# Low parts of the weights made earlier in DVE's order around three seams of a hybrid decoder layer

## The chip, the cores and the metric

The kernel runs on one core of one Trainium2 chip. The metric is device time in microseconds (us) of one execution; the figure of record before the change is 2464.99 us, the median of 3 runs (2464.16 to 2465.22).

## The reference

One inference step of one decoder layer with two branches, on 512 prompt tokens and 64 sample tokens (576 columns), width 2048, all in float32:

```python
h = rmsnorm(x, norm_g)
proj = einsum('bld,dp->blp', h, w_in)          # gates, conv inputs, q, k, v, forget code
za = cB * conv3(cC * cx) * silu(cg)            # branch A: short gated conv
branch_a = einsum('blc,cd->bld', za, w_branch_a)
o, S_new = gla_chunked(q, k, v, log_a, state)  # branch B: gated linear attention
zb = rmsnorm(o, gla_norm_g) * silu(gg)
branch_b = einsum('blv,vd->bld', zb, w_branch_b)
merged = sigmoid(ga) * branch_a + sigmoid(gb) * branch_b
x = x + einsum('bld,de->ble', merged, w_out)
y = rmsnorm(x, final_norm_g)
```

## The kernel before

TensorE computes everything in float32 by splitting each operand in a rounded high part and the remaining low part, and by taking three passes: high x high, high x low, low x high.

The first 715 us or so hold the attention work. What follows is the **pair stage**: 76 pairs of output tiles. Each pair is computed with a seven-product scheme of the Strassen kind (`NPROD = 7`), so there are 532 products, numbered `g = 7 * u + p` (u is the pair, p the product in it). Each product is 8 k-tiles times 3 passes, 24 matmuls of 128x128 by 288 columns. The pairs come in four phases:

- pairs 0 to 51: the projection, whose operand is h;
- pairs 52 to 59 (from `PAIR_A` = 52): branch A, `w_branch_a`;
- pairs 60 to 67 (from `PAIR_B` = 60): branch B, `w_branch_b`, with the merge;
- pairs 68 to 75 (from `PAIR_C` = 68): the output product, `w_out`.

At each of the three **seams** (52, 60, 68) the operand on the token side changes: seven new operand blocks are loaded or made, and ACT and DVE split them while the products run. In the first pair of a phase TensorE waits later than elsewhere (`late`): it starts a product with the high parts alone, and needs the weights' low part after 8 matmuls and a new operand's low part after 16. In all other pairs a product needs the weights' low part at its start.

The weights of product g go this way. SP loads four pieces of a pair (a11, a21, a12, a22). For p = 1, 2, 4, 5 DVE adds or subtracts two pieces first (`add_pieces`, L1973, L1978, L1980, L1982). ACT rounds the piece to its high part (`split_hi`, L1087) into a ring of three buffers; a buffer comes free when product g - 3 is done. DVE subtracts to get the low part (`split_lo`, L1963). Piece buffers come free when the low part is made, and SP waits for that count (`part_lo`) before it loads the next pair's pieces.

All engines run their orders as written. ACT's order for iteration g: save a product of the pair from PSUM (`save`, L1289), then `split_hi(g + 2)`, then splits of operands (L1417, L1345) and, around branch B, `slice_hi` (L1327), which waits for what DVE's stage made (`c_made`). Products 2, 4, 5 and 6 of a pair wait until an earlier product of it is saved (`part_saved`).

DVE's order for iteration g, while TensorE runs product g:

1. the stage's arithmetic on product g - 1, for p - 1 from 3 to 6 (`branch_a` L2470 to L2487, `branch_b` L2508 to L2546, `out_pair` L2588, L2591);
2. `add_pieces(g + 3)`, where that product needs a sum;
3. `split_lo(g + 2)`;
4. low parts of new operands (L2652; at seam C `rest_lo`, L2572), slices of branch B (L2553, L2560), the output rows (L2600).

In the output phase `turn_out` puts five transposes on TensorE in front of product 1 of each pair from 69 on; they wait for the stage's arithmetic on product 5 of the pair before (`c12_read`).

Of the kernel before, what the change touches and what calls it, by code (L numbers as in the profile page):

```python
# [46 lines left out]
NPROD = len(PRODUCTS)  # L47
# [22 lines left out]
PAIR_A, PAIR_B, PAIR_C = PAIRS_G, PAIRS_G + PAIRS_B, PAIRS_G + 2 * PAIRS_B  # L70
# [13 lines left out]
C_LO = ((2, 0, 3, 7), (4, 1, 0, 7), (5, 0, 7, 8), (6, 1, 7, 8), (7, 2, 7, 8), (8, 3, 0, 8), (9, 4, 7, 8), (10, 5, 0, 8),  # L84
        (11, 6, 0, 8))
# [4 lines left out]
NG = NPAIR * NPROD  # L90

def hybrid_kernel(nc, x_prompt, x_sample, state_conv, state_gla, norm_g, w_in, conv_w, w_alpha2,
# [51 lines left out]
    with ctx:  # L144
# [305 lines left out]
        def slot_of(slot, b, f32=False):  # L450

            if isinstance(slot, int):
                return (x_f32 if f32 else act_x)[:, slot, 1 - b, :, :]
            kh, j = int(slot[1]) - 1, int(slot[2]) - 1
            return (y_f32 if f32 else act_y)[:, kh * KH:(kh + 1) * KH, b, j * HALF:(j + 1) * HALF]
# [6 lines left out]
        def split_count(f, p):  # L462


            return 4 + NPROD * f + list(SPLITS[f].values()).index(p) + 1

        def phase_of(u):

            return (u >= PAIR_A) + (u >= PAIR_B) + (u >= PAIR_C)
# [22 lines left out]
        def kind_of(u):  # L492

            return FIRST[u][0] if u < PAIR_A else "branch" if u < PAIR_C else "out"
# [12 lines left out]
        def closed_before(u):  # L507

            return sum(closing[:u])
# [1343 lines left out]
        def _(dve):  # L1853
# [57 lines left out]
            for t in range(NT + 1):  # L1911
# [9 lines left out]
                n = P if t < NT else TS  # L1921
# [37 lines left out]
            def split_lo(g):  # L1959

                u, p = g // NPROD, g % NPROD
                dve.wait_ge(part_hi, g + 1)
                V.tensor_tensor(ring_lo[g % RING][:, :], piece_of[SOURCE[p]][u % 2][:, :],  # L1963
                                ring_hi[g % RING][:, :].bitcast(F32), ALU.subtract).then_inc(part_lo, 1)

            def add_pieces(g):

                u, p = g // NPROD, g % NPROD
                a11, a21, a12, a22 = (piece_of[name][u % 2][:, :] for name in ("a11", "a21", "a12", "a22"))
                if p == 1:  # L1970
                    dve.wait_ge(piece_in["a21"][0], 16 * (u + 1))
                    dve.wait_ge(piece_in["a22"][u % 2], 16 * (u // 2 + 1))
                    ins = V.tensor_tensor(a21, a21, a22, ALU.add)  # L1973
                else:
                    dve.wait_ge(w_sum, sums_before(g) - 1)
                    dve.wait_ge(part_lo, u * NPROD + {2: 1, 4: 2, 5: 4}[p])
                if p == 2:
                    ins = V.tensor_tensor(a11, a11, a21, ALU.add)  # L1978
                if p == 4:
                    ins = V.tensor_tensor(a21, a11, a22, ALU.subtract)  # L1980
                if p == 5:
                    ins = V.tensor_tensor(a12, a12, a11, ALU.add)  # L1982
                ins.then_inc(w_sum, 1)
# [27 lines left out]
            def x_low(q):  # L2011

                V.tensor_tensor(act_x[:, q, 0, :, :], x_f32[:, q, 0, :, :], act_x[:, q, 1, :, :].bitcast(F32),
                                ALU.subtract).then_inc(x_lo, 1)
# [365 lines left out]
            def conv_tails(u):  # L2380


                m = FIRST[u][1]
                tails = tail_c.rearrange("p (k r) -> p k r", r=2 * NS + 2)
                state = state_c.rearrange("p (k s r) -> p k s r", s=NS, r=2)
                for n in range(2):
                    ins = V.tensor_copy(u_smp[:, n, :, 0:2], state[:, m + n * KH, :, :])
                    V.tensor_copy(tails[:, m + n * KH, 0:2], u_row[:, n, TP:TP + 2])
                    ins = V.tensor_copy(tails[:, m + n * KH, 2:].rearrange("p (s r) -> p s r", r=2),
                                        u_smp[:, n, :, LS:LS + 2])  # L2390
                ins.then_inc(tail_ready, 1)
# [164 lines left out]
            def first_slice_lo(m):  # L2556

                dve.wait_ge(x_hi, 4 + 2 * NPROD + m + 1)
                slot = SLOTS[3][0]
                V.tensor_tensor(slot_of(slot, 1)[:, m, :], made_at(m, 0), slot_of(slot, 0)[:, m, :].bitcast(F32),  # L2560
                                ALU.subtract).then_inc(x_lo, 1)

            def rest_lo(n):


                _, p, k0, k1 = C_LO[n]
                slot = SLOTS[3][p]
                src = slot_of(slot, 1, True)[:, k0:k1, :]
                if p == 0 and k1 == KH:
                    src = e1[:, :].rearrange("p (k t) -> p k t", k=1)  # L2570
                dve.wait_ge(x_hi, 4 + 2 * NPROD + MADE + [c[1:] for c in C_HI].index(C_LO[n][1:]) + 1)
                V.tensor_tensor(slot_of(slot, 1)[:, k0:k1, :], src, slot_of(slot, 0)[:, k0:k1, :].bitcast(F32),  # L2572
                                ALU.subtract).then_inc(x_lo, 1)
# [29 lines left out]
            def weight(m, tiles, count):  # L2603
# [3 lines left out]
                g = out_rows[:, place(m), OUT_N:].rearrange("p (o c) -> p o c", o=1).to_broadcast([P, len(tiles), 2 * P])  # L2607
                V.tensor_tensor(dst, dst, g, ALU.mult).then_inc(weighted, 1)

            first = {"c": conv_c, "x": conv_x, "b": conv_b, "g": close_add, "o": close_add, "ga": gates, "gb": gates}  # L2610
            dve.wait_ge(half_saved, NH)
            V.memset(u_row[:, :, 0:2], 0.0)
            for u in range(NPAIR):
                kind = kind_of(u)
                last = kind_of(u - 1) if u else "branch"
                for p in range(NPROD):
                    g = u * NPROD + p
                    v, q = (u, p - 1) if p else (u - 1, NPROD - 1)
                    if g and q >= 3:
                        stage = (branch_a, branch_b, out_pair)[phase_of(v) - 1] if v >= PAIR_A else first[FIRST[v][0]]  # L2620
                        stage(v, q)
                    if (g + 3) % NPROD in (1, 2, 4, 5) and g and g + 3 < NG:
                        add_pieces(g + 3)
                    if g + 2 < NG:
                        split_lo(g + 2)
                    if g == 0:
                        dve.wait_ge(x_hi, 4)
                        x_low(3)
                    if kind == "b" and p == 0:
                        if u == 2:  # L2630
                            dve.wait_ge(c_in, 32)
                        conv_tails(u)
                        dve.wait_ge(tail_ready, FIRST[u][1] + 1)
                        if u > 4:
                            dve.wait_ge(z_out, 48 * closed_before(u))
                        conv_y(u, 0, False)
                    if kind == "b" and p in (1, 2):
                        conv_y(u, p - 1, p == 1)
                    if kind == "b" and p == 3:
                        conv_y(u, 1, True).then_inc(conv_done, 1)  # L2640
                    if kind in ("g", "o") and p >= 5:
                        close_mult(u, p - 2)
                    if last in ("g", "o") and p < 2:
                        close_mult(u - 1, p + 5)
                    if last in ("g", "o") and p == 1:
                        close_sums(u - 1)
                    for h, start in ((1, PAIR_A), (2, PAIR_B)):
                        q = SPLITS[h - 1].get(g - (start - 1) * NPROD)
                        if q is not None:
                            slot = SLOTS[h][0 if q in AHEAD[h - 1] else q]  # L2650
                            dve.wait_ge(x_hi, split_count(h - 1, q))
                            V.tensor_tensor(slot_of(slot, 1), slot_of(slot, 1, True), slot_of(slot, 0).bitcast(F32),  # L2652
                                            ALU.subtract).then_inc(x_lo, 1)
                    m = u - PAIR_B
                    if 0 < m <= MADE and p == 0:
                        first_slice_lo(m - 1)
                    if 0 < m < PAIRS_B and p == 0:
                        slice_lo(u - 1, 4)
                    if 0 < m < PAIRS_B and p == 1:
                        slice_lo(u - 1, 2)  # L2660
                    for n, c in enumerate(C_LO):
                        if g - (PAIR_C - 1) * NPROD == c[0]:
                            rest_lo(n)
                    m = u - 1 - PAIR_C
                    if m >= 0 and p in (1, 3):
                        add_rows(m, p // 2)
                    if m >= 0 and p == 6:
                        weight(m, range(NT + 1), m + 1)
# [100 lines left out]
```

## Time and profile before

| | |
|---|---|
| median of 3 runs | 2464.99 us (2464.16 to 2465.22) |
| the profiled execution, its own time | 2462.21 us |
| its span in the profile | 2460.3 us |
| TensorE (PE) busy | 2417.9 us, 98% |
| weight loads (PEld) busy | 2367.8 us, 96% |
| DVE busy | 1852.6 us, 75% |
| ACT busy | 1073.7 us, 44% |
| granted TensorE clock, mean | 0.997 |

The profiled execution took 1.9 us more than its span and 2.8 us less than the median of the runs. PE is the matmul, PEld the weight load that runs beside it; a gap in PEld is what a product started too late by. In timelines a row is a start, a duration and a line of the kernel, and the bracket says how long the engine sat idle before it and what released it.

### The profile page before, as it was taken

How to read it: one execution, taken by the hardware profiler on the slowest of the kernel's cores; microseconds unless marked ns; L12 is line 12 of the kernel's file. 1: busy time of each engine (PE TensorE's matmuls, PEld its weight loads, DVE VectorE, ACT ScalarE, POOL GpSimd, SP SyncE). 2: the span in 40 equal slices, each digit the busy share in tenths (PEclk: the TensorE clock that was granted, in tenths of full speed). 3: DMA queues.
4: the chain of work that ended last, by engine and by line, in shares of the span. 5: the costliest groups of instructions: out<-in, count | busy, mean ns of one | idle time of the engine just before them, and what ended most of it. 6: DMA issues, size and time to landing. Idle time of an engine off the chain costs nothing.

```text
span 2460.3 us, 43963 instructions
## 1 busy us (share of the span) xinstructions
PE 2417.9 (98%) x18106; PEld 2367.8 (96%) x18106; DVE 1852.6 (75%) x2718; ACT 1073.7 (44%) x1620; POOL 277.6 (11%) x474
## 2 busy tenths in 40 slices
PE   8999999999999999999999999999999999999996
PEld 7998989999899999999999999999999999998996
DVE  7457667575687787878878878876677778989775
ACT  6343444434443443443444344444445445445443
POOL 3002121020200000000000011100000110332111
PEclk9999999999999999999999999999999999999998
DMA  7325344252533443343433445654579668669555
GB/s 204 86 61 173 110 130 153 82 191 71 193 103 94 120 120 93 97 121 103 111 103 96 130 132 159 172 147 131 159 206 284 217 215 291 197 196 296 143 149 161
DMA packets 456248, 369.03 MB, mean 150 GB/s; under 512 B 15989, under 2 KB 425761, under 8 KB 453537
## 3 DMA queue, kind: packets, MB, share of 16 engines
q1 hardware_dynamic: 419826, 238.91, 35.0%
q0 software_dynamic: 36224, 127.32, 15.6%
q8 instruction: 144, 2.36, 0.4%
q14 instruction: 54, 0.44, 0.1%
HBM read 286.50 MB, written 79.68 MB: 149 GB/s over the span
## 4 chain that ended last, share of the span: by engine, by line
PE 91%; DVE 3%; DMA 2%; issue 2%; ACT 1%; POOL 0%; SPq 0%; ACTq 0%; DVEq 0%; POOLq 0%
PE bank L1842 36%; PE acc L1842 28%; PE acc L1699 20%; PE acc L1655 1%; DVE ring_lo L1963 1%; PE acc L1584 1%; PE bank L1652 1%; PE bank L1628 1%; PE bank L1616 1%; PE bank L1649 1%; DMA x_rows<-in_x_prompt 0%; DMA x_f<-zw_d 0%; DMA pa<-in_w_branch_a 0%; PE bank L1571 0%; PE acc L1752 0%
## 5 line engine op out<-in xcount | busy, mean ns | idle before, releaser
L1963 DVE TENSOR_TENSOR ring_lo<-pa,ring_hi 128x1024 fp32r<-128x1024 f32 x532 | 650.0, 1222 | 201.6 <-ACT ring_hi L1087 198.5
L1087 ACT ACTIVATE ring_hi<-pa 128x1024 fp32r<-128x1024 f32 x532 | 561.6, 1056 | 375.5 <-PE bank L1842 218.9
L1699 PE MATMUL acc<-act_y,w_hi 128*128 128x288 f32 x2560 | 519.8, 298 | 0.0
L1842 PE MATMUL bank<-act_y,ring_hi 128*128 128x288 f32 x2432 | 478.3, 295 | 1.9 <-DMA act_y<-zs_d 1.1
L1842 PE MATMUL bank<-act_x,ring_hi 128*128 128x288 f32 x2432 | 475.7, 294 | 2.1 <-ACT act_x L1345 1.2
L1842 PE MATMUL acc<-act_x,ring_hi 128*128 128x288 f32 x2176 | 435.3, 294 | 1.3 <-DVE ring_lo L1963 1.3
L1699 PEld LDWEIGHTS acc<-act_y,w_hi 128*128 128x128 f32 x2560 | 411.0, 189 | 2.6 <-issue 1.2
L1842 PEld LDWEIGHTS bank<-act_x,ring_hi 128*128 128x128 f32 x2432 | 387.5, 189 | 3.0 <-ACT act_x L1345 1.7
L1842 PEld LDWEIGHTS bank<-act_y,ring_hi 128*128 128x128 f32 x2432 | 385.1, 189 | 3.1 <-DMA act_y<-zs_d 1.4
L1699 PE MATMUL acc<-act_y,w_lo 128*128 128x288 f32 x1280 | 377.9, 295 | 0.0
L1842 PEld LDWEIGHTS acc<-act_x,ring_hi 128*128 128x128 f32 x2176 | 351.1, 189 | 1.5 <-issue 1.5
L1842 PE MATMUL bank<-act_x,ring_lo 128*128 128x288 f32 x1216 | 344.5, 296 | 0.6 <-DVE ring_lo L1963 0.5
L1842 PE MATMUL bank<-act_y,ring_lo 128*128 128x288 f32 x1216 | 342.8, 295 | 0.0
L1842 PE MATMUL acc<-act_x,ring_lo 128*128 128x288 f32 x1088 | 322.4, 296 | 0.0
L1842 PE MATMUL acc<-act_y,ring_hi 128*128 128x288 f32 x1472 | 295.7, 295 | 3.8 <-DVE ring_lo L1963 3.8
L1699 PEld LDWEIGHTS acc<-act_y,w_lo 128*128 128x128 f32 x1280 | 242.0, 189 | 0.0
L1842 PEld LDWEIGHTS acc<-act_y,ring_hi 128*128 128x128 f32 x1472 | 236.0, 189 | 4.7 <-issue 4.4
L1842 PEld LDWEIGHTS bank<-act_x,ring_lo 128*128 128x128 f32 x1216 | 222.7, 188 | 1.0 <-DVE ring_lo L1963 1.0
L1842 PEld LDWEIGHTS bank<-act_y,ring_lo 128*128 128x128 f32 x1216 | 223.2, 188 | 0.0
L1842 PE MATMUL acc<-act_y,ring_lo 128*128 128x288 f32 x736 | 217.1, 295 | 0.0
L1842 PEld LDWEIGHTS acc<-act_x,ring_lo 128*128 128x128 f32 x1088 | 204.1, 188 | 0.0
L1289 ACT ACTIVATE part<-acc 128x288 f32<-128x288 f32 x152 | 62.5, 411 | 264.1 <-PE acc L1842 264.0
(365 smaller groups left out, 2700.1 us busy)
## 6 DMA issues: line engine op xcount, KB each, us to landing
pa<-in_w_in SPq DMA_DIRECT2D x208, 512.0 KB, 5.3
raw<-in_w_in SPq DMA_DIRECT2D x40, 1024.0 KB, 5.6
pa<-in_w_branch_a SPq DMA_DIRECT2D x32, 512.0 KB, 5.9
pa<-in_w_branch_b SPq DMA_DIRECT2D x32, 512.0 KB, 7.0
pa<-in_w_out SPq DMA_DIRECT2D x32, 512.0 KB, 6.8
states<-in_state_gla POOLq DMA_DIRECT2D x48, 256.0 KB, 3.3
out<-states POOLq DMA_DIRECT2D x48, 256.0 KB, 2.5
zt_d<-gate_tile POOLq DMA_DIRECT2D x12, 576.0 KB, 3.5
```

Of the source, the lines that this page charges most:

```text
L1087: A(ring_hi[g % RING][:, :], piece_of[src][u % 2][:, :], ACT.Copy).then_inc(part_hi, 1)
L1289: A(dst[:, :], psum_of(u)[b], ACT.Copy).then_inc(part_saved, 1)
L1584: mm = nc.tensor.matmul(b_gram[:, a * P:(a + 1) * P], dec[:, kk, a * P:(a + 1) * P], dec[:, kk, MID + a * P:MID + (a + 1) * P], start=(kk ...
L1616: nc.tensor.matmul(b_smp[r:r + TS // 2, :], q_pad[:, a % 2, kk, b, :], state_of(2 * a + b)[:, kk, :], start=(a == 0), stop=(a == NS // 2 - 1))
L1628: mm = nc.tensor.matmul(bank[:, kk, :], kd_one[:, kk * P:(kk + 1) * P], v2[:, j // (NS // 2), :], start=True, stop=True)
L1649: nc.tensor.matmul(out, v_rows[:, b, v * P:(v + 1) * P], scores[:, b * P:(b + 1) * P], start=True, stop=(c == 0))
L1652: nc.tensor.matmul(out, s_prompt[:, kk, v * P:(v + 1) * P], qe[:, kk, b * P:(b + 1) * P], start=False, stop=(kk == KK - 1))
L1655: mm = nc.tensor.matmul(b_chunk[kk], kd_rows[:, b, kk * P:(kk + 1) * P], v_rows[:, b, :], start=True, stop=True)
L1699: mm = nc.tensor.matmul(half_bank[h % 2][:, 0:HALF], (w_hi, w_lo)[a][par][:, k * P:(k + 1) * P], y_of(k, b, j), start=(k == 0 and n == 0), ...
L1842: mm = nc.tensor.matmul(out, (ring_hi, ring_lo)[a][r][:, k * P:(k + 1) * P], slot_of(slot, b)[:, k, :], start=(p in (0, 1, 3) and k == 0 a ...
L1963: V.tensor_tensor(ring_lo[g % RING][:, :], piece_of[SOURCE[p]][u % 2][:, :], ring_hi[g % RING][:, :].bitcast(F32), ALU.subtract).then_inc( ...
```

## The change

In eleven iterations at each seam, from the last product of the pair before it to the third product of the pair after its first one, DVE does `split_lo(g + 2)` as the first thing of the iteration, ahead of the stage's arithmetic and of `add_pieces(g + 3)`. In the first pair after seam C, from its second product on, the operand low parts `rest_lo` move ahead as well, right behind `split_lo`. No instruction is added or removed, and only DVE's order changes.

```diff
+            def low_part_first(g):
+                return any(NPROD * start - 1 <= g < NPROD * (start + 1) + 3 for start in (PAIR_A, PAIR_B, PAIR_C))
+
+            def rest_lows(g):
+                for n, c in enumerate(C_LO):
+                    if g - (PAIR_C - 1) * NPROD == c[0]:
+                        rest_lo(n)
...
                     v, q = (u, p - 1) if p else (u - 1, NPROD - 1)
+                    if low_part_first(g):
+                        split_lo(g + 2)
+                    if g > NPROD * PAIR_C:
+                        rest_lows(g)
                     if g and q >= 3:
                         stage = (branch_a, branch_b, out_pair)[phase_of(v) - 1] if v >= PAIR_A else first[FIRST[v][0]]
                         stage(v, q)
                     if (g + 3) % NPROD in (1, 2, 4, 5) and g and g + 3 < NG:
                         add_pieces(g + 3)
-                    if g + 2 < NG:
+                    if g + 2 < NG and not low_part_first(g):
                         split_lo(g + 2)
...
-                    for n, c in enumerate(C_LO):
-                        if g - (PAIR_C - 1) * NPROD == c[0]:
-                            rest_lo(n)
+                    if g <= NPROD * PAIR_C:
+                        rest_lows(g)
```

## Rows read from the trace of the kernel before

**Rows 1.** The page: busy time by engine, and the chain that ended last.
```profile
PE 2417.9 (98%) x18106; PEld 2367.8 (96%) x18106; DVE 1852.6 (75%) x2718; ACT 1073.7 (44%) x1620; POOL 277.6 (11%) x474
...
PE 91%; DVE 3%; DMA 2%; issue 2%; ACT 1%; POOL 0%; SPq 0%; ACTq 0%; DVEq 0%; POOLq 0%
```

**Rows 2.** Matmuls of the pair stage (L1842): idle before them (us, times), by releaser.
```profile
  DVE ring_lo L1963: 6.6, 7
```

**Rows 3.** Timeline of PEld at the three seams: starts that came late.
```profile
1905.86 0.30 PEld L1842 LDWEIGHTS acc<-act_y,ring_hi 128*128 128x128 f32 x2 [1.04 <-issue]
...
2079.91 1.10 PEld L1842 LDWEIGHTS bank<-act_y,ring_hi 128*128 128x128 f32 x8 [0.25 <-DVE act_y L2652]
...
2086.08 0.30 PEld L1842 LDWEIGHTS acc<-act_x,ring_hi 128*128 128x128 f32 x2 [1.53 <-issue]
2091.07 0.30 PEld L1842 LDWEIGHTS acc<-act_y,ring_hi 128*128 128x128 f32 x2 [1.77 <-issue]
...
2264.27 1.10 PEld L1842 LDWEIGHTS bank<-act_x,ring_hi 128*128 128x128 f32 x8 [1.39 <-ACT act_x L1345]
...
2270.83 1.10 PEld L1842 LDWEIGHTS bank<-act_y,ring_hi 128*128 128x128 f32 x8 [0.74 <-DVE act_y L2572]
2273.53 0.30 PEld L1842 LDWEIGHTS acc<-act_y,ring_hi 128*128 128x128 f32 x2 [1.60 <-issue]
```

**Rows 4.** Timeline of DVE at seam B.
```profile
2072.93 1.22 DVE L1982 TENSOR_TENSOR pa<-pa,pa 128x1024 f32<-128x1024 f32 x1
...
2077.29 2.56 DVE L2652 TENSOR_TENSOR act_y<-y_f,act_y 128x2304 fp32r<-128x2304 f32 x1 [0.79 <-ACT act_y L1417]
...
2083.61 1.22 DVE L1973 TENSOR_TENSOR pa<-pa,pa 128x1024 f32<-128x1024 f32 x1
...
2088.60 1.22 DVE L1978 TENSOR_TENSOR pa<-pa,pa 128x1024 f32<-128x1024 f32 x1
2089.74 1.22 DVE L1963 TENSOR_TENSOR ring_lo<-pa,ring_hi 128x1024 fp32r<-128x1024 f32 x1
...
2092.22 1.22 DVE L1963 TENSOR_TENSOR ring_lo<-pa,ring_hi 128x1024 fp32r<-128x1024 f32 x1
...
2112.11 1.22 DVE L1963 TENSOR_TENSOR ring_lo<-pa,ring_hi 128x1024 fp32r<-128x1024 f32 x1
```

**Rows 5.** Timeline of ACT at seam B.
```profile
2075.15 2.11 ACT L1417 ACTIVATE act_y<-y_f 128x2304 fp32r<-128x2304 f32 x1
...
2084.87 1.06 ACT L1087 ACTIVATE ring_hi<-pa 128x1024 fp32r<-128x1024 f32 x1 [3.18 <-DVE pa L1973]
...
2092.34 0.45 ACT L1327 ACTIVATE gate_r<-y_f 128x288 fp32r<-128x288 f32 x1 [1.43 <-DVE y_f L2546]
2092.69 0.39 ACT L1289 ACTIVATE part<-acc 128x288 f32<-128x288 f32 x1
```

**Rows 6.** Timeline of ACT at seam A.
```profile
1916.06 1.05 ACT L1087 ACTIVATE ring_hi<-pa 128x1024 fp32r<-128x1024 f32 x1
```

**Rows 7.** Timeline of DVE at seam A.
```profile
1903.38 1.22 DVE L1973 TENSOR_TENSOR pa<-pa,pa 128x1024 f32<-128x1024 f32 x1 [1.42 <-DMA pa<-in_w_branch_a]
...
1917.15 1.22 DVE L1963 TENSOR_TENSOR ring_lo<-pa,ring_hi 128x1024 fp32r<-128x1024 f32 x1 [1.94 <-ACT ring_hi L1087]
```

**Rows 8.** Timeline of DVE at seam C.
```profile
2247.29 1.22 DVE L1978 TENSOR_TENSOR pa<-pa,pa 128x1024 f32<-128x1024 f32 x1
...
2255.05 2.55 DVE L2572 TENSOR_TENSOR act_y<-y_f,act_y 128x2304 fp32r<-128x2304 f32 x1
```

**Rows 9.** Timeline of ACT at seam C.
```profile
2251.73 2.14 ACT L1345 ACTIVATE act_y<-y_f 128x2304 fp32r<-128x2304 f32 x1 [0.89 <-DMA y_f<-zw_d]
...
2262.09 2.12 ACT L1345 ACTIVATE act_x<-x_f 128x2304 fp32r<-128x2304 f32 x1 [2.26 <-DMA x_f<-zw_d]
...
2280.78 0.41 ACT L1289 ACTIVATE part<-acc 128x288 f32<-128x288 f32 x1 [2.37 <-PE acc L1842]
```

## The prediction

> **What bounds the kernel now.** I read the page first: TensorE is busy 98% of the span and stands for 91% of the chain that ended last [rows 1]. So the span moves only with TensorE's own gaps. Then I asked what sits idle before the pair stage's matmuls: the weights' low part accounts for 6.6 us in 7 places [rows 2]. That is all that an earlier low part could give back, 0.27% of the time. Last I read the timelines of PEld, DVE and ACT around each seam. The reader should see where the seven places lie (the largest four: 1.04 at seam A, 1.53 and 1.77 at seam B, 1.60 at seam C [rows 3]) and that other gaps beside them have other causes (0.25 and 0.74 for an operand's low part, 1.39 for its high part [rows 3]).
>
> I call the products of a seam's first pair F0 to F6 and those of the next pair G0 to G6. TensorE takes 3.2 us for a product: G1 at seam B began at 2091.07, after G0 at 2086.08, with 1.77 of idle between [rows 3].
>
> **The tools for the sums.** From a sum's start to the start of its rounding on ACT: 1.26 (2083.61 to 2084.87 [rows 4, 5]). From a rounding's start to its low part, if DVE is free: 1.09 [rows 6, 7]. From a low part's start to the product that waits for it: 1.33 (2089.74 to 2091.07 [rows 3, 4]). A sum or a low part holds DVE for 1.13 (2088.60 to 2089.74 [rows 4]). The chain sum, rounding, low part, product is therefore 3.68 long, and the ring is three deep.
>
> **What the change moves.** Nothing is added or removed, so DVE's own 1.13 per low part costs nothing in total. Each low part comes earlier by the work in front of it; the stage's arithmetic and the next sum come later by 1.13, and by more where DVE now waits for ACT. That wait is new. In the old order DVE filled the 1.26 + 1.09 from a sum to its low part with the next stage's arithmetic. In the new one the low part stands right behind the sum that its own rounding needs, so DVE idles up to 1.2 each time, with the arithmetic and the next sum queued behind it. ACT's later roundings, its operand splits and its saves wait for those. SP's piece loads are released by low parts, so they are issued up to 1.1 earlier, and no product here waits longer for them; POOL's stores and gate loads hang on the arithmetic and come 1 to 5 us later, still ahead of their users by my walk, so I cost both at nothing. I walked each seam with the prices above and all other spacings as they stand.
>
> **Seam A.** The low part of G0 no longer stands behind sum G1, which waited until 1903.38 for its piece [rows 7]: the 1.04 goes. G1's sum starts no earlier than 1903.38, or slightly earlier if its piece, asked for 1.1 sooner, lands sooner. Then rounding G1 1904.63, low part 1905.72, arithmetic of F5 (0.86) from 1906.86, sum G2 1907.72, rounding 1908.97, low part 1910.06, G2 on TensorE 1911.39. TensorE is ready for it at 1904.82 + 6.4 = 1911.2. Loss 0.15. **Seam A: -0.9** (bounds -1.04 to +0.5).
>
> **Seam B.** Two steps lose.
>
> First, the sum of F5 stands behind the low part of F4 and moves from 2072.93 [rows 4] to 2074.15. ACT rounds F5 at 2075.40 and only then, 0.96 later, splits the operand of F5: 2076.36 instead of 2075.15 [rows 5]. DVE's half of that split moves from 2077.29 [rows 4] to 2078.50, and the third pass of F5 from 2079.91 [rows 3] to 2081.1. That is +1.2. From there F6 runs without its own small wait, and G0 starts at 2085.4 against 2086.08: the 1.53 is gone, half of it paid back already.
>
> Second, the arithmetic of branch B is long: 2.71 for F5 (from 2083.61, a sum and a low part of 1.13 or 1.14 each and then the arithmetic, to 2088.60) and 1.35 for F6 (between the low parts at 2089.74 and 2092.22 [rows 4], less 1.13). DVE now runs: low part F6 2080.97, arithmetic F3 to 2083.46, low part G0, arithmetic F4 to 2085.94, sum G1; rounding 2087.19; low part G1 2088.28, and G1 on TensorE 2089.6 instead of 2091.07. Then the arithmetic of F5 to 2092.13, sum G2, rounding 2093.38, low part G2 2094.47, so G2 could start at 2095.8. But ACT stands in front of it. Its order there is `slice_hi`, which waits for the arithmetic of F6, and behind that the save of G0, without which G2 may not start. Before: 2092.34 and 2092.69 [rows 5]. Now the arithmetic of F6 is behind low part G2 and ends at 2097.04, so the slice is at 2097.08, the save 2097.43 to 2097.84, and G2 starts at 2097.9. Before, it started at 2091.07 + 3.2 = 2094.3. **+3.6.**
>
> Afterwards DVE is behind. It waits for ACT again before the low parts of G3, G4 and G5, and reaches the arithmetic of G3 2.3 later against TensorE than before; 0.9 of that is slack there. In the second pair after the seam the low part of product 1 was made at 2112.11 [rows 4], ready at 2113.44, when TensorE wanted it at 2094.3 + 6 x 3.2 = 2113.5: no slack. I take 1.2 more. **Seam B: +4.8** (bounds +1.2, if only the operand's step stays, to +7, if the lag is paid in one more pair).
>
> **Seam C.** The sum of F2 moves from 2247.29 [rows 8] to 2248.3, rounding 2249.5, low part 2250.6, and the arithmetic of pair 67's last product behind it ends at 2253.17. ACT's split of F3's operand needs that: 2253.20 instead of 2251.73 [rows 9]. The moved `rest_lo` starts at 2255.37 instead of 2255.05 [rows 8] and holds 2.47, and sum F4 is now behind it: 2257.84, rounding 2259.09, low part 2260.18, 0.37 for a small `rest_lo` behind it, sum F5 2261.69, rounding 2262.94. ACT splits F5's operand at 2263.90 instead of 2262.09 [rows 9]: the 1.39 gap [rows 3] becomes about 2.4 there, with F4 itself 0.5 late. F6's third pass comes at 2272.3 instead of 2270.83 [rows 3] and G0 at 2273.84 instead of 2273.53 [rows 3], because its low part is ready when needed. G1 waits for its sum (2274.01), rounding (2275.26), low part (2276.35) and then for the transposes in front of it, which need the arithmetic of F5, now behind that low part: it ends at 2277.94, the transposes take 0.5, and G1 starts at 2278.5. Before, the save behind G1 was at 2280.78 [rows 9], which puts G1 at 2277.3. **Seam C: +1.2** (bounds -0.5 to +2.5).
>
> Sum: -0.9 + 4.8 + 1.2 = **+5.1**. The profiled execution's 2462.21 becomes 2467.3; the median stands 2.78 above it, so 2464.99 + 5.1 = **2470.1 us**.
>
> Against this stands a rule of the Trainium skill (Perfetto Trace Analysis, Optimization Strategy): find the gaps on the engine that should be saturated, find what each waits for, and make that dependency start sooner or end faster. The change does just that, and by the rule the sum would be the 6.6 of the low parts alone; the walk above says that the dependency's own input, the sum, starts later. No row of before shows the new order.
>
> **Rivals.**
> - *It works as meant*: the low-part waits go (-6.6 [rows 2]) and the later sums are absorbed by the ring. 2458.4 us. For it: a product is 3.2 and the ring holds three. Against: the chain is 3.68 and DVE at seam B has 4.06 of arithmetic for two products. It decides if G2 at seam B starts before 2094.3. Chance 0.10.
> - *Gains and losses nearly cancel*: G2 at seam B waits for its low part alone (+1.5) and the next pair absorbs the lag, or the pieces at seam A land sooner. -0.9 + 1.5 + 1.2 gives 2466.8 us. Chance 0.38, from 0 to +4.9.
> - *It spreads*: every branch B pair has no slack at product 1, so DVE's lag is paid in several. +9 or more, 2474 us and up. Against: DVE sits idle in each pair before the arithmetic of product 3. Chance 0.10.
>
> **How the numbers follow.** The walk's own case, +4.9 to +8, has 0.42. A difference of 0.2%, 4.9 us, is about what can be told from no change here, and the sum lies on that border. Slower: 0.42 and 0.10 give 0.52; same 0.38; faster 0.10. The range leaves out the rival that works as meant and most of the spreading one: 2463 to 2475.
>
> **What would show it.** DVE's waits for the rounding (low part L1963 after L1087) appear at G1 and G2. At seam B the save L1289 of G0 stands at about 2097.4 behind L1327 and G2 has some 5 us of gap before it; a gap of about 1.2 sits before product 1 of pair 62. At seam A the gap before G0 is gone. At seam C L1345 stands at 2253.2 and 2263.9. It would be wrong if the save is not what G2 waits for, or if sums start earlier than I place them.

## The result, and the profile after

The changed kernel takes 2469.32 us (median of 18 runs, 2468.23 to 2471.02). The kernel before, on the same chips, takes 2464.43 us (18 runs, 2462.62 to 2468.21). The ratio is 1.0020, with a 95% interval of 1.0014 to 1.0027: slower by 4.9 us. The forecast was +5.1 us and 2470.1 us. One run of a kernel further down (seam C alone, 2943.59 us at a granted clock of 0.752) is left out of its median.

The page of the changed kernel, the span, the busy times and the chain:

```profile
span 2467.1 us, 43963 instructions
...
PE 2420.7 (98%) x18106; PEld 2371.1 (96%) x18106; DVE 1852.9 (75%) x2718; ACT 1073.5 (44%) x1620; POOL 277.4 (11%) x474
...
PE 91%; DVE 3%; DMA 2%; issue 1%; ACT 1%; SPq 0%; POOL 0%; ACTq 0%; DVEq 0%; POOLq 0%
```

DVE has the same work (1852.9 us against 1852.6 [rows 1]) and TensorE's share of the chain is the same. Two things differ: TensorE is busy 2.8 us longer with the same matmuls (the clock, below), and the gaps between its matmuls are others. The idle time ahead of the pair stage's matmuls by releaser, in the changed kernel:

```profile
  ACT part L1289: 12.8, 3
...
  DVE ring_lo L1963: 1.1, 2
```

The change did what it says. The waits for the weights' low part fell from 6.6 us [rows 2] to 1.1 us. A new releaser has their place, the save of a product by ACT. The 12.8 counts a gap of the matmuls and the same gap of the weight loads both, so it is not time lost; the gaps themselves stand below.

The two profiled executions differ by 6.8 us and the medians by 4.9, so the reader should first see how much of it is not the change. I compare the start of the same save of a product, before seam A, after it, after seam B and after seam C, in the kernel before:

```profile
1868.69 0.41 ACT L1289 ACTIVATE part<-acc 128x288 f32<-128x288 f32 x1 [1.82 <-PE acc L1842]
...
1938.00 0.41 ACT L1289 ACTIVATE part<-bank 128x288 f32<-128x288 f32 x1 [1.64 <-PE bank L1842]
...
2206.46 0.41 ACT L1289 ACTIVATE part<-bank 128x288 f32<-128x288 f32 x1 [0.57 <-PE bank L1842]
...
2300.39 0.41 ACT L1289 ACTIVATE part<-bank 128x288 f32<-128x288 f32 x1 [1.86 <-PE bank L1842]
```

and in the changed kernel:

```profile
1869.14 0.41 ACT L1289 ACTIVATE part<-acc 128x288 f32<-128x288 f32 x1 [1.82 <-PE acc L1842]
...
1937.60 0.41 ACT L1289 ACTIVATE part<-bank 128x288 f32<-128x288 f32 x1 [1.64 <-PE bank L1842]
...
2211.74 0.41 ACT L1289 ACTIVATE part<-bank 128x288 f32<-128x288 f32 x1 [0.57 <-PE bank L1842]
...
2307.21 0.41 ACT L1289 ACTIVATE part<-bank 128x288 f32<-128x288 f32 x1 [1.86 <-PE bank L1842]
```

The differences are +0.45, -0.40, +5.28 and +6.82. So seam A gave -0.85, seam B +5.68, seam C +1.54, and 0.45 was there before any seam. I use these four marks for every run below; what stands before seam A is start-up and varies from -0.2 to +4.9 between executions, so a whole span from one profile says little here.

The late starts of weight loads in the changed kernel (idle time in brackets):

```profile
1901.98 1.09 PEld L1842 LDWEIGHTS bank<-act_y,ring_hi 128*128 128x128 f32 x8 [1.16 <-DMA act_y<-zs_d]
...
1911.81 0.30 PEld L1842 LDWEIGHTS acc<-act_x,ring_hi 128*128 128x128 f32 x2 [0.27 <-issue]
...
2078.14 1.09 PEld L1842 LDWEIGHTS bank<-act_y,ring_hi 128*128 128x128 f32 x8 [1.01 <-ACT act_y L1417]
2080.73 1.10 PEld L1842 LDWEIGHTS bank<-act_y,ring_hi 128*128 128x128 f32 x8 [0.43 <-DVE act_y L2667]
...
2089.26 0.30 PEld L1842 LDWEIGHTS acc<-act_y,ring_hi 128*128 128x128 f32 x2 [1.05 <-issue]
2097.52 0.50 PEld L1842 LDWEIGHTS acc<-act_y,ring_hi 128*128 128x128 f32 x2 [5.06 <-ACT part L1289]
...
2254.31 1.10 PEld L1842 LDWEIGHTS bank<-act_x,ring_hi 128*128 128x128 f32 x8 [1.46 <-ACT act_x L1345]
...
2267.70 0.43 PEld L1842 LDWEIGHTS bank<-act_x,ring_hi 128*128 128x128 f32 x3 [3.11 <-issue]
2279.34 0.30 PEld L1842 LDWEIGHTS acc<-act_y,ring_hi 128*128 128x128 f32 x2 [0.47 <-issue]
2283.56 0.53 PEld L1752 LDWEIGHTS acc<-ident,gate_tile 128*128 128x128 f32 x5 [1.03 <-issue]
```

The 1.04 and 1.53 ahead of G0 at seams A and B [rows 3] are gone, and of the 1.60 at seam C 0.47 is left. New are 5.06 ahead of G2 at seam B and 3.11 ahead of F4 at seam C, and two smaller ones that matter below: 1.01 ahead of F5 at seam B and 1.03 ahead of the transposes in front of G1 at seam C (L1752). DVE and then ACT ahead of that G2:

```profile
2091.77 1.22 DVE L1978 TENSOR_TENSOR pa<-pa,pa 128x1024 f32<-128x1024 f32 x1
2094.11 1.22 DVE L1963 TENSOR_TENSOR ring_lo<-pa,ring_hi 128x1024 fp32r<-128x1024 f32 x1 [1.12 <-ACT ring_hi L1087]
...
2096.23 0.46 DVE L2546 SCALAR_TENSOR_TENSOR y_f<-y_f 128x288 f32<-128x288 f32 x1
```

```profile
2096.72 0.44 ACT L1327 ACTIVATE gate_r<-y_f 128x288 fp32r<-128x288 f32 x1 [2.64 <-DVE y_f L2546]
2097.07 0.39 ACT L1289 ACTIVATE part<-acc 128x288 f32<-128x288 f32 x1
```

Low part G2 starts at 2094.11 and would let G2 go at 2095.4. But the save of G0 stands behind the slice, which waits for the end of the arithmetic of F6, now behind that low part. The save ends at 2097.46 and G2 starts at 2097.52.

What I had not seen coming is TensorE's clock. Busy times by stretch in the changed kernel, for PE, PEld, DVE, ACT and POOL (number of instructions in brackets), then the granted clock, the DMA share and GB/s:

```profile
2092.00:2097.00 5.00, 0.69 (x6) 0.46 (x4) 3.81 (x7) 1.66 (x3) 0.72 (x1) 0.82 0.18 59
2097.00:2099.00 2.00, 1.48 (x6) 1.48 (x7) 0.98 (x3) 1.71 (x4) 1.09 (x2) 0.50 0.08 32
2099.00:2101.00 2.00, 2.00 (x10) 2.00 (x9) 2.00 (x3) 0.16 (x1) 0.72 (x1) 0.50 0.64 226
2101.00:2103.00 2.00, 2.00 (x14) 2.00 (x13) 1.24 (x2) 0.90 (x1) 1.51 (x3) 0.75 0.31 111
2103.00:2105.00 2.00, 2.00 (x17) 2.00 (x16) 1.29 (x2) 1.08 (x2) 1.02 (x3) 1.00 0.64 179
```

In the long gap the clock falls to 0.50, the lower of its two levels (1.2 GHz), and stays there for most of G2: 10 matmuls in 2 us where it does 17 at 1.00. G2 takes 5.28 us (2097.52 to 2102.80, where G3's first matmul starts) instead of 3.2. The Trainium skill (Perfetto Trace Analysis, Matmul Optimizations) says that the matmul engine scales power by utilization, so that matmuls should run back to back; these rows agree, and what they don't tell is which gaps do it (last section).

### The profile page after: what moved, and what is told of

Its sections match the earlier page's. It is cut to its first block, busy times and chain, and to the rows that moved or that the text cites. A ratio compares the mean times of both kernels' runs of the same rounds, so it can differ in the third digit from the quotient of the medians.

```text
span 2467.1 us, 43963 instructions
## 1 busy us (share of the span) xinstructions
PE 2420.7 (98%) x18106; PEld 2371.1 (96%) x18106; DVE 1852.9 (75%) x2718; ACT 1073.5 (44%) x1620; POOL 277.4 (11%) x474
## 4 chain that ended last, share of the span: by engine, by line
PE 91%; DVE 3%; DMA 2%; issue 1%; ACT 1%; SPq 0%; POOL 0%; ACTq 0%; DVEq 0%; POOLq 0%
PE bank L1842 36%; PE acc L1842 28%; PE acc L1699 20%; PE acc L1655 1%; PE acc L1584 1%; PE bank L1652 1%; DVE ring_lo L1963 1%; DMA act_y<-zs_d 1%; DMA x_rows<-in_x_prompt 1%; PE bank L1628 1%; PE bank L1616 1%; PE bank L1649 1%; DMA mix_tile<-ma_d 0%; PE bank L1571 0%; PE acc L1752 0%
## 5 line engine op out<-in xcount | busy, mean ns | idle before, releaser
L1842 PE MATMUL bank<-act_y,ring_hi 128*128 128x288 f32 x2432 | 478.6, 296 | 2.1 <-DMA act_y<-zs_d 0.9
L1842 PE MATMUL bank<-act_x,ring_hi 128*128 128x288 f32 x2432 | 476.4, 295 | 4.1 <-ACT part L1289 2.9
L1842 PE MATMUL acc<-act_x,ring_hi 128*128 128x288 f32 x2176 | 435.2, 294 | 0.1
L1842 PEld LDWEIGHTS bank<-act_x,ring_hi 128*128 128x128 f32 x2432 | 388.6, 190 | 4.7 <-issue 3.1
L1842 PEld LDWEIGHTS bank<-act_y,ring_hi 128*128 128x128 f32 x2432 | 385.1, 189 | 3.5 <-DMA act_y<-zs_d 1.2
L1842 PEld LDWEIGHTS acc<-act_x,ring_hi 128*128 128x128 f32 x2176 | 351.1, 189 | 0.3 <-issue 0.3
L1842 PE MATMUL bank<-act_x,ring_lo 128*128 128x288 f32 x1216 | 344.9, 297 | 0.0
L1842 PE MATMUL bank<-act_y,ring_lo 128*128 128x288 f32 x1216 | 342.9, 295 | 0.0
L1842 PE MATMUL acc<-act_x,ring_lo 128*128 128x288 f32 x1088 | 322.4, 296 | 0.0
L1842 PE MATMUL acc<-act_y,ring_hi 128*128 128x288 f32 x1472 | 297.5, 297 | 5.9 <-ACT part L1289 4.8
L1842 PEld LDWEIGHTS acc<-act_y,ring_hi 128*128 128x128 f32 x1472 | 237.6, 190 | 6.8 <-ACT part L1289 5.1
L1842 PEld LDWEIGHTS bank<-act_x,ring_lo 128*128 128x128 f32 x1216 | 223.3, 188 | 0.0
L1842 PEld LDWEIGHTS bank<-act_y,ring_lo 128*128 128x128 f32 x1216 | 223.3, 188 | 0.0
L1842 PE MATMUL acc<-act_y,ring_lo 128*128 128x288 f32 x736 | 217.9, 296 | 0.0
L1842 PEld LDWEIGHTS acc<-act_x,ring_lo 128*128 128x128 f32 x1088 | 204.1, 188 | 0.0
```

The lines of the kernel that those rows point to most:

```text
L1842: mm = nc.tensor.matmul(out, (ring_hi, ring_lo)[a][r][:, k * P:(k + 1) * P], slot_of(slot, b)[:, k, :], start=(p in (0, 1, 3) and k == 0 a ...
```

## The experiments

Eleven kernels were run. All medians below are against the kernel before, run beside them on the same chip (2464.19 to 2465.16 us). Each interval reaches some 2.2 us to either side, so where two kernels differ by 1 or 2 us the difference rests on their traces.

**The seams one by one.** The change with its list of seams cut to one:

```
e1:  ... for start in (PAIR_A,))      # operand low parts in their old place
e2:  ... for start in (PAIR_B,))      # operand low parts in their old place
e3:  ... for start in (PAIR_C,))
```

Seam A alone:

> The change at seam A alone. By the forecast's walk this is its only winning part: -0.9 us against the kernel before, with the 1.04 us start of G0 gone and the clock at 1.00 throughout. If the loss of the whole change came from transfers that are asked for earlier (rival), seam A, where DMA is busiest, would lose 1 us or more.

Seam B alone:

> The change at seam B alone. The trace of the changed kernel puts +5.7 us between the stretches before and after this seam: +3.6 of gaps ahead of G2 and some 2.1 of G2's own matmuls at a granted clock of 0.50. Queue and clock theory: +5 to +6 us against the kernel before, a gap of about 5 us ahead of G2. The forecast's own sum: +4.8, of which 1.2 at product 1 of pair 62. If the seams act on each other the figure is other than 5.7.

Seam C alone:

> The change at seam C alone, the moved low parts of operands with it. The changed kernel's trace shows +1.5 us here, with a gap of 3 us ahead of F4 and the clock at 0.50 behind it. Theory: +1.5 us (1 to 2.5). The forecast's sum: +1.2 without any fall of the clock.

Measured: A alone 2464.12 us (0.9994, interval 0.9985 to 1.0004), B alone 2469.85 (1.0018, 1.0009 to 1.0028), C alone 2465.20 (1.0000, 0.9990 to 1.0009). The medians' differences are -1.0, +4.7 and 0.0; they add up to +3.7, and the whole change is +4.9. In the traces the marks give -1.03, +5.15 and +1.57 for the seam that each changes. So seam B loses about all, and seams do not act on each other by more than the noise. Only B's median is clear of no change; that A wins rests on its trace, where the 1.04 is gone. The rival for A, earlier transfers, fell: no loss of 1 us shows.

How far the marks can be trusted, the same traces show at the seams that an edit left alone: -0.20 and -0.29 at A, +0.08 and +0.04 at B, but +1.32 (A alone) and +0.30 (B alone) at C. For seam C trace (+1.57) and median (0.0) differ, within the interval; one reason can be read in the rows. In the kernel before, F4 waits for a transfer for 0.90 in the profiled execution; in other kernels whose order at seam C is as before it waited 1.16 (B alone) and 2.13 (A alone), about the +0.30 and +1.32 just named. In the changed kernel the longer wait ahead of F4 covers that transfer. The profiled execution of the kernel before happened to have a short one.

**The save ahead of the slice.** The changed kernel, ACT's order in pair 61:

```diff
                         save(u, 1, e1, 0)
+                        if u == PAIR_B + 1:
+                            slice_hi(u - 1, 2)
...
-                    if 0 < m < PAIRS_B and p == 0:
+                    if 0 < m < PAIRS_B and p == 0 and not (u == PAIR_B + 1):
                         slice_hi(u - 1, 2)
```

> The changed kernel, with one step of ACT's order turned round in the pair after seam B: the save of G0 stands ahead of the slice that waits for the arithmetic of F6. If the queue on ACT holds G2 (theory), G2 starts 2.1 us earlier, when its low part is ready, and the time is at least 2 us below the changed kernel's; 4 us below if the shorter gap also leaves the clock alone. If G2 waits for its low part or for DVE alone (rival), nothing changes.

Measured: 2468.26 us (1.0011, 1.0001 to 1.0020), +3.1, so 1.8 below the changed kernel and not the 2 or more that were expected; seam B by the marks +4.51 instead of +5.68. Late starts at seam B, and the clock behind G2's start:

```profile
2094.94 0.30 PEld L1844 LDWEIGHTS acc<-act_y,ring_hi 128*128 128x128 f32 x2 [2.97 <-issue]
2098.98 0.30 PEld L1844 LDWEIGHTS bank<-act_x,ring_hi 128*128 128x128 f32 x2 [0.82 <-issue]
...
2117.05 0.30 PEld L1844 LDWEIGHTS bank<-act_y,ring_hi 128*128 128x128 f32 x2 [1.51 <-issue]
```

```profile
2095.00:2097.00 2.00, 2.00 (x15) 2.00 (x16) 1.85 (x5) 0.79 (x2) 0.00 (x0) 1.00 0.00 0
```

The gap ahead of G2 is 2.97 instead of 5.06, so the queue on ACT did hold G2 by 2.1 us. The clock stays at 1.00. But only 1.2 of the 4 us that both together could give comes back: G3 (0.82) and product 1 of pair 62 (1.51) are late now, for DVE's low part. The second is the wait that the forecast had (1.2) and that the changed kernel did not show.

**Idle work in the gaps.** To part the clock from the gap:

```diff
+                    for _ in range({(PAIR_B + 1, 2): 36, (PAIR_C, 4): 18}.get((u, p), 0)):
+                        nc.tensor.transpose(acc[1][:, 0:P], ident[:, :], ident[:, :])
                     if p in (2, 4, 5, 6):
                         pe.wait_ge(part_saved, ...)
```

> The changed kernel with idle transposes on TensorE (36 ahead of G2 at seam B, 18 ahead of F4 at seam C) inside the two long gaps, their results unused. Clock theory: the granted clock stays at 1.00 behind both gaps; seam B gives back the 2.1 us of G2's slow matmuls, but then DVE's lag shows at product 1 of pair 62 (1.2 to 1.5 us, as in the run with the save first), and seam C gives back 1.5 us. In all 2 to 2.5 us below the changed kernel. Rival, the gaps alone are the loss: the transposes change nothing or cost time.

Measured: 2469.20 us (1.0018, 1.0009 to 1.0027), +5.0: no gain. By the marks seam B +4.89 instead of +5.68 and seam C +1.56 instead of +1.54. Clock and late starts:

```profile
2097.00:2099.00 2.00, 1.28 (x9) 1.29 (x10) 0.98 (x3) 1.91 (x4) 1.07 (x2) 1.00 0.00 0
...
2268.00:2270.00 2.00, 2.00 (x18) 2.00 (x17) 1.04 (x1) 2.00 (x2) 0.00 (x0) 1.00 0.88 266
```

```profile
2097.71 0.30 PEld L1844 LDWEIGHTS acc<-act_y,ring_hi 128*128 128x128 f32 x2 [1.10 <-ACT part L1289]
2118.05 0.30 PEld L1844 LDWEIGHTS bank<-act_y,ring_hi 128*128 128x128 f32 x2 [1.20 <-issue]
...
2271.00 1.09 PEld L1844 LDWEIGHTS bank<-act_x,ring_hi 128*128 128x128 f32 x8 [0.83 <-ACT act_x L1345]
...
2282.98 0.53 PEld L1752 LDWEIGHTS acc<-ident,gate_tile 128*128 128x128 f32 x5 [1.02 <-issue]
```

The transposes held the clock at 1.00 behind both gaps. At seam B the 2.1 of slow matmuls went, and 1.20 came up at product 1 of pair 62, as expected: 0.8 net. At seam C my expectation fell: F5 is late for its operand (0.83), and the transposes in front of G1 wait 1.02 for DVE, as they waited 1.03 in the changed kernel. TensorE reaches G1 no earlier, whatever it did at F4. The slow clock is real, but it runs beside DVE's and ACT's lag, and whichever is longer counts.

**The operands' low parts back behind the sums** (seam C):

```diff
-                    if g > NPROD * PAIR_C:
-                        rest_lows(g)
...
-                    if g <= NPROD * PAIR_C:
-                        rest_lows(g)
+                    rest_lows(g)
```

> The changed kernel with the operands' low parts of the first pair after seam C back behind the sums. Theory: at seam C sum F4 no longer waits behind an operand's low part, so the rounding of F4 and the saves behind it on ACT come some 3 us earlier, the 3.1 us gap ahead of F4 is gone and with it the slow clock: 1.5 to 2 us below the changed kernel, seam C at -0.5 against the kernel before. Rival, the late sum F2 and the slice behind it set seam C: no change at F4.

Measured: 2467.97 us (1.0017, 1.0008 to 1.0026), +3.8. The 3.11 ahead of F4 is gone and the clock is 1.00 in every stretch of seam C. But the marks give seam C +1.77. What F4 waits for now:

```profile
2268.62 1.10 PEld L1842 LDWEIGHTS bank<-act_x,ring_hi 128*128 128x128 f32 x8 [2.17 <-DMA act_x<-zp_d]
```

It is the transfer, 2.17 against 0.90 in the profiled execution before; the mark less these 1.27 leaves 0.5, and -0.5 was expected. The expected gain of 1.5 to 2 is 1.1 by the medians. The transposes in front of G1 wait 1.03 here too. So the moved `rest_lo` explains the gap ahead of F4; that it explains the seam's loss is not shown.

**The low part of G2 alone in its old place** (all three seams): `and g != NPROD * (start + 1)` in the condition.

> The changed kernel with the low part of G2 alone back behind the arithmetic of F6 (all three seams). Theory: at seam B the arithmetic of F6 runs while ACT rounds G2, the slice and the save of G0 are done before G2's low part is, and G2 starts at the low part: gap 2.8 us instead of 5.1, clock at 1.00, DVE's lag smaller by the 1.1 us that it waited. Seam B at +3 instead of +5.7, so 2 to 3 us below the changed kernel. The rest of the loss is then the low part of G1 ahead of the arithmetic of F5 and sum G2.

Measured: 2467.36 us (1.0015, 1.0006 to 1.0024), +3.2. Seam B by the marks +2.51; the gap ahead of G2:

```profile
2100.24 0.30 PEld L1842 LDWEIGHTS acc<-act_y,ring_hi 128*128 128x128 f32 x2 [3.13 <-ACT part L1289]
```

The gap is a little longer than expected (3.13 for 2.8), the clock stays at 1.00 there, and the seam is near the +3 expected. By the marks more than half of seam B's loss is that one low part ahead of the arithmetic of F6; the medians give 1.7 of 4.9.

**The other order: sums first.** From the kernel before, five iterations:

```diff
+    {NPROD * PAIR_A + 5: ("low", "stage", "sum"), NPROD * PAIR_C + 5: ("low", "stage", "sum"),
+     NPROD * PAIR_B + 5: ("low", "sum", "stage"), NPROD * PAIR_B + 6: ("sum", "low", "stage"),
+     NPROD * PAIR_B + 7: ("low", "stage")}.get(g, ("stage", "sum", "low"))
```

and on ACT the save ahead of the slice, as above.

> The kernel before with five iterations in another order. Seams A and C: the low part of G0 ahead of the arithmetic of F4 and of sum G1. Seam B: low part G0, sum G1, arithmetic F4; then sum G2, low part G1, arithmetic F5; then low part G2, arithmetic F6; and on ACT the save of G0 ahead of the slice. Theory (what TensorE waits for at seam B is the sum two steps up, behind 2.7 us of arithmetic): A -1.0, B -2.0 to -2.6, C -1.1, in all 4 to 4.7 us below the kernel before. Rival (DVE's total work bounds seam B, whatever its order): B gives nothing, 2 us in all.

Measured: 2462.49 us (0.9995, 0.9986 to 1.0004), -1.7, which alone is not clear of no change; marks A -1.37, B +1.03, C -1.43. A and C as expected (both had a shorter transfer wait by 0.2 to 0.4), B not. ACT ahead of G2 at seam B, and the clock behind:

```profile
2089.60 0.44 ACT L1327 ACTIVATE gate_r<-mix_tile 128x288 fp32r<-128x288 f32 x1 [5.27 <-DVE y_f L2539]
2089.95 1.04 ACT L1087 ACTIVATE ring_hi<-pa 128x1024 fp32r<-128x1024 f32 x1
```

```profile
2094.00:2095.00 1.00, 1.00 (x6) 1.00 (x6) 1.00 (x2) 1.00 (x3) 0.36 (x1) 0.50 0.00 0
```

The sum of G2 was done at 2085.7, but its rounding stood behind the other slice, which waits for the arithmetic of F5. G2 came 2.19 late and then ran at 0.50.

**Slices behind the roundings.** The same kernel with that slice behind the rounding of G2 (e9), and then with the second slice behind the rounding of G3 too, and low part G3 ahead of sum G4 (e10). The lines of e10 stand against the kernel before; the second slice, an iteration later, is there behind the save of G0 as well:

```diff
 e9, on ACT
-                    if 0 <= m < PAIRS_B - 1 and p == 6:
+                    if 0 < m < PAIRS_B - 1 and p == 6:
                         slice_hi(u, 4)
+                    if m == 1 and p == 0:
+                        slice_hi(u - 1, 4)
 e10, on ACT and DVE
-                    if 0 < m < PAIRS_B and p == 0:
+                    if 0 < m < PAIRS_B and p == (m == 1):
                         slice_hi(u - 1, 2)
+     NPROD * PAIR_B + 8: ("low", "sum")
```

> The kernel with the sums first and one more step turned round on ACT: the first slice of pair 60, which waits for the arithmetic of F5, stands behind the rounding of G2 instead of ahead of it. In the run before it held that rounding until 2089.95 though its sum was done at 2085.8. Queue theory: the low part of G2 moves to 2089.5, the 2.2 us gap ahead of G2 shrinks to 0.7, the clock stays at 1.00 behind it: 3 us below the run before at seam B, some 4 to 5 us (0.2%) below the kernel before in all. Rival, DVE's work bounds seam B: G2 waits as long for its low part.

Measured: 2461.41 us (0.9988, 0.9979 to 0.9997), -3.4; seam B by the marks -0.24.

```profile
2092.31 0.30 PEld L1846 LDWEIGHTS acc<-act_y,ring_hi 128*128 128x128 f32 x2 [0.65 <-ACT part L1289]
2096.67 0.30 PEld L1846 LDWEIGHTS bank<-act_x,ring_hi 128*128 128x128 f32 x2 [1.13 <-issue]
```

The gap ahead of G2 is 0.65 as expected and the clock stays at 1.00. The wait moved on to G3, so seam B gained 1.3 on the run before, and not 3. The other marks are -1.11 at A and +0.07 at C, where F4 waited 1.85 for its transfer against 0.90.

> The kernel of the run before, with both slices of pair 60 behind ACT's roundings (of G2 and of G3), and on DVE the low part of G3 ahead of sum G4. In the run before G3 came 1.1 us late: its rounding stood behind the second slice, its low part behind the arithmetic of F6 and sum G4. Queue theory: that gap goes, seam B gives another 1 us, 4 to 5 us below the kernel before in all. Rival, DVE's work bounds the seam: the wait moves on to G4 or G5 and nothing is gained.

Measured: 2460.62 us (0.9983, 0.9975 to 0.9992), -3.8. Seam B -1.34 by the marks, C -0.75, and A +0.33: in this execution an operand's transfer at seam A was late (ACT waited 2.37 for it, against 0.90 in the last run below) and a product waited 0.94 behind it.

```profile
2092.61 0.30 PEld L1844 LDWEIGHTS acc<-act_y,ring_hi 128*128 128x128 f32 x2 [0.64 <-ACT part L1289]
2099.61 0.30 PEld L1844 LDWEIGHTS acc<-act_x,ring_hi 128*128 128x128 f32 x2 [0.57 <-issue]
```

As expected the gap ahead of G3 is gone; 0.57 came up ahead of G4, which is the rival in part. This is the lowest median of the study, 0.17% below the kernel before, a little short of the 4 to 5 us expected; against the -3.4 of the run before it is not told apart.

**Two iterations alone.** Of the five iterations with another order, those of seams A and C alone, with ACT as before:

> The kernel before with the low part first in two iterations alone, product 5 of the first pair at seams A and C (the low part of G0 ahead of the arithmetic of F4 and sum G1). Theory: these are the two places where the low part is late and nothing that is pushed back is waited for: -1.0 at A and -1.1 at C, 2 us below the kernel before, at the edge of what can be measured; the trace should show both gaps gone and no new one over 0.5 us.

Measured: 2462.19 us (0.9989, 0.9980 to 0.9998), -2.3; marks A -1.11, B +0.03, C -0.64 (with a transfer wait ahead of F4 of 1.27 against 0.90). The gap ahead of G0 is gone at both seams, and one of 0.40 ahead of G1 at seam C is new:

```profile
2276.07 0.30 PEld L1842 LDWEIGHTS acc<-act_x,ring_hi 128*128 128x128 f32 x2 [0.40 <-issue]
```

## Why the prediction was right, step by step

- **Total, +5.1.** Measured +4.9. That it fits to 0.2 us is in part luck: at seam B a term of 1.2 did not show and a cost of 2.1 that the sum did not have stood in its place, and the marks of the one profiled pair give +6.4 for the three seams together.
- **Seam A, -0.9.** The marks show -0.85 in the changed kernel and -1.03 with A alone, the medians -1.0 (interval -3.7 to +1.0). Right by the traces, G2's small gap included (0.15 said, 0.27 seen).
- **Seam B, the operand of F5, +1.2.** The third pass came at 2080.73; corrected by the -0.40 of that trace, it is 1.2 later than before [rows 3]. Right. Most of the wait stood one step earlier than I wrote, ahead of F5's first pass (1.01, for the high part on ACT), which I had not checked.
- **Seam B, G1 and G2.** With the same -0.40: G1 expected at 2089.2, seen at 2089.26; save of G0 at 2097.0, seen at 2097.07; G2 at 2097.5, seen at 2097.52. Right, and the run with the save first shows that ACT's queue and not the low part held G2.
- **Seam B, 1.2 at product 1 of pair 62.** This term failed as the changed kernel shows it. There is no such gap. In its place G2 ran at the low clock and cost 2.1. With the clock held (transposes) the gap appears, 1.20, and seam B's mark is +4.89 for the +4.8 said. So DVE's lag was sized right, and what failed is that the sum had no clock: B +5.7 by the marks.
- **Seam C, +1.2.** The marks show +1.54, the medians 0.0 for C alone. ACT's splits came where I put them: 2258.72 and 2269.42, less the 5.28 of shift, are 2253.44 and 2264.14, for 2253.20 and 2263.90. But the walk missed a step. ACT at seam C in the changed kernel:

```profile
2264.61 1.06 ACT L1087 ACTIVATE ring_hi<-pa 128x1024 fp32r<-128x1024 f32 x1 [3.13 <-DVE pa L1980]
2265.68 1.28 ACT L1430 ACT_TABLE_LOAD   x1
...
2267.09 0.39 ACT L1289 ACTIVATE part<-bank 128x288 f32<-128x288 f32 x1
```

  The late sum F4 makes the rounding of F4 late, behind it stands a table load of 1.28, and behind that the save that F4 itself needs. I let F4 start with its rounding, 0.5 late; it started with the save, after a gap of 3.11. This step costs nothing at the seam's end, because TensorE then waits less for F5, F6 and G0, and what counts is the walk's last step. DVE at the end of the seam:

```profile
2279.51 1.22 DVE L1973 TENSOR_TENSOR pa<-pa,pa 128x1024 f32<-128x1024 f32 x1
2281.85 1.23 DVE L1963 TENSOR_TENSOR ring_lo<-pa,ring_hi 128x1024 fp32r<-128x1024 f32 x1 [1.13 <-ACT ring_hi L1087]
2282.99 0.45 DVE L2591 TENSOR_TENSOR gate_tile<-bank,part 128x288 f32<-128x288 f32 x1
```

  Less the shift, sum G1 is at 2274.23 (said 2274.01), low part G1 at 2276.57 (2276.35), and the arithmetic of F5 behind it ends at 2278.1 (2277.94). The transposes in front of G1 wait for it, 1.03, and start at 2278.28. They start within 0.02 us of that, corrected the same way, in the kernels with C alone, with the save first, with idle transposes and with the low part of G2 back, and the mark is +1.54 to +1.57 in each, whether the clock fell behind F4's gap or was held. So this term was right by its mechanism, and its missing step had no price.
- **SP and POOL at nothing.** Nothing in the traces speaks against it: seam A, with the most transfers, gained what the walk said.
- **Rivals.** "Works as meant" has its condition refuted: G2 started at 2097.5 and not before 2094.3. "It spreads" did not happen: the marks after seam B stay at +5.28 until seam C. The measured +4.9 lies on the border between the walk's case and the one that nearly cancels, as the text said it would.

What stays open: how much seam C loses against a kernel before with a usual transfer. The traces have +1.54 to +1.57 five times, against one execution of the kernel before whose transfer ahead of F4 was short; C alone has 0.0 by the medians, with an interval of about 2.2 us to each side.

## What to carry to other kernels

When one engine makes both the input of a step and its output, with another engine in between, moving the output's step to the front moves the input of the next one back; walk the whole ring, other engines' queues included, before counting the wait that goes. Here the same idea in two iterations instead of 33 gives -2.3 us, and with the sums first and ACT's slices behind its roundings -3.8 us. A save or a rounding that TensorE waits for shouldn't stand behind an instruction that waits for slow arithmetic, and where a wait is taken away the trace of the next run shows which one was hiding behind it.

## What the runs showed of the hardware that was not expected

- The granted clock falls to 0.50 in and behind some gaps of TensorE, and not others, so the length of the one gap does not tell which. It fell in the 5.06 gap at seam B (G2 then took 5.28 us instead of 3.2), behind the 3.11 gap at seam C, and behind a gap of 2.19 ahead of G2 with one of 0.62 ahead of G1 (sums first). It stayed at 1.00 behind the 2.97 gap of the run with the save first and behind the 3.13 of the run with the low part of G2 in its old place, though both had one of 1.05 ahead of G1.
- What the same gap costs varies: behind 5.06 us ahead of G2, G2 took 5.28 us in the changed kernel, 5.09 with the operands' low parts back behind the sums, and 4.78 with B alone (2098.00 to 2102.78), where the clock fell only as G2 began (granted 0.98 from 2096 to 2098).
- Filling a gap with transposes kept the clock at 1.00 and was worth 0.8 us at one seam and nothing at the other, since the slow stretch ran beside work that was late anyway.
- The table load on ACT (`ACT_TABLE_LOAD`) takes 1.28 us, and all that ACT has behind it waits, the save for F4 among it.
